# Scores of a local attention in one fp32 pass or in three fp32r passes, 128 or 256 keys wide

## The chip, the cores and the metric

The kernel runs on one core of a Trainium2 chip. The metric is the device time of one execution in microseconds (us). Engines are called by the names of the profile: PE is TensorE, PEld its weight load, DVE is VectorE, ACT is ScalarE, POOL is GpSimd, SP is SyncE, which here issues DMA transfers. Each engine works through its own list of instructions in order. They wait for each other by semaphores.

## The reference, cut to what matters

The program computes two transformer blocks, one after the other, on 512 tokens of width 1024. The first block has a gated mixer with a delta rule, cross attention over 256 memory rows and an MLP. The second block starts with eight projections of the same normalised input, among them q (8 heads of 64), k and v (2 heads of 64). The change is in its local attention:

```
q = apply_rope(q.reshape(b, s, 8, 64), cos, sin)
k = apply_rope(k.reshape(b, s, 2, 64), cos, sin)
# 4 blocks of 128 queries; each sees its own 128 keys and the 128 before them
scores = einsum('bnqhgd,bnkhd->bnhgqk', qb, kk) * 64 ** -0.5
scores = where(band & not_pad, scores, -inf)
m = maximum(max(scores), sink)
p = exp(scores - m);  denom = sum(p) + exp(sink - m)
out = einsum('bnhgqk,bnkhd->bnqhgd', p / denom, vv)
```

Beside it run a convolution branch (projections cb, cc, cx) and the gates. All products with weights are made in three passes over high and low parts: an fp32 number x is split into x_hi (rounded to fp32r) and x_lo = x - x_hi, and hi*hi + lo*hi + hi*lo is added up in one PSUM bank.

## The kernel before, in words

`schedule()` writes the order of all steps by hand as one list of (kind, number). Every engine walks through this list and does its own part of each kind, so a step's place in the list is its place on every engine that it touches.

Weights come as units of up to eight 128x128 tiles. For unit j, SP loads the raw weights, the step `split` makes w_hi on ACT (L1574), `low` makes w_lo on DVE (L1867), and `mm` is 24 matmuls of 128x512 on PE (L1272 to L1274). A split stands in the list three units ahead of its mm. The result lies in one of four PSUM banks until DVE takes it out (L1851, "leave").

Around the change the units are k2, q2 0, v2, q2 1 to 3, then cc2, cx2 and cb2 for each of eight tiles. After q2 n is out, ACT adds its bias (step `leave_q`, L1770), `rotate` n makes the rotated half in four copies on ACT (L1779, L1780), and `turned` n multiplies and adds on DVE (L2228, L2229, L2232). Two heads of each of the two key groups lie in one tile q2[:, n, :]: partitions 0 to 63 hold the head of group 0, partitions 64 to 127 that of group 1. k2 is one such tile.

`scores` n is one of 16 steps: PAIRS gives (block, pair, group), so that steps come in twos, one for each group. PE does both groups of a batch at the first of the two: for the two heads i of the pair and both groups, one fp32 matmul (L1530) of 64 partitions by 128 queries against 128 keys (block 0) or 256 keys (blocks 1 to 3). There are 8 such batches, of 4 matmuls each, and the trace records each fp32 matmul as two. DVE then adds the mask, takes the maximum and adds the sink (L2253 to L2262), ACT takes Exp (L1794, L1797) and DVE sums and inverts (L2264, L2266). Pairs 0 and 1 of the q2 tiles are tiles 0, 1 and tiles 2, 3. So batch 1 (scores 0 and 1) needs q2 0 and 1, and batch 2 (scores 2 and 3) needs q2 2 and 3. Batch 1 stands after mm cx2 0, batch 2 after mm cc2 1, with mm cb2 0 between them. PE waits with `turned_dve` before a batch.

Of the kernel before, what the change touches and what calls it, by code (L numbers as in the profile page):

```python
# [8 lines left out]
F32 = mybir.dt.float32  # L9
# [6 lines left out]
P = 128  # L16
# [177 lines left out]
def schedule():  # L194
# [3 lines left out]
    def add(kind, n=0):  # L198
        out.append((kind, n))
# [223 lines left out]
    for n in range(1, QT):  # L423
        project("q2", n)
        add("leave_q", n)
        if n == 1:
            add("value_turn")
        else:
            add("rotate", n - 1)
        if n != 2:  # L430
            add("turned", n // 2)

    def window_attention():
        for g in range(KVH):
# [14 lines left out]
    def conv_branch():  # L449
        for n in range(KT):  # L450
            project("cc2", n)
            add("cc", n)
            if n == 0:
                add("rotate", QT - 1)
                add("turned", QT - 2)
            yield
            project("cx2", n)
            add("cx", n)
            if n == 0:
                add("turned", QT - 1)  # L460
            yield
            project("cb2", n)
            add("cb", n)
            add("normed", n)
            add("b", (B_CONV, n))
            yield
        for n in range(KT):
            project("gc2", n)
            add("gate_c", n)
            yield  # L470
            project("conv_out2", n)
            add("conv_out", n)
            yield
# [282 lines left out]
def build_program(nc, x_in, mem_in, front_in, logits_in, weights_in, ws_in, columns_in, rows_in, sinks_in, matrices_in,  # L756
                  positions_in, out):
    with ExitStack() as base:
# [23 lines left out]
        sinks = sbuf("sinks", [P, QH])  # L782
        matrices = sbuf("matrices", [P, N_MATRICES, P])
        rstd = sbuf("rstd", [P, S])
        square_sum = sbuf("square_sum", [P, S])
        squares = [sbuf(f"square{i}", [P, S]) for i in range(2)]
        narrow = sbuf("narrow", [P, 16, H * NC])
        wide = [sbuf(f"temp{i}", [P, PAD + S]) for i in range(5)]
# [5 lines left out]
        k_low, v_low = ExitStack(), ExitStack()  # L794
        mem_k_lo = [sbuf("mem_k_early_lo", [P, EARLY_KEYS, M], F32R, stack=k_low)]
        k_low.close()
        mem_k_early = sbuf("mem_k_early", [P, EARLY_KEYS, M])
        banks = [base.enter_context(nc.psum_tensor(f"bank{i}", [P, S], F32)) for i in range(8)]

# [50 lines left out]
        second = ExitStack()  # L850
        rope_cos = sbuf("rope_cos", [P, S], stack=second)
        rope_sin = sbuf("rope_sin", [P, S], stack=second)
        q2 = sbuf("q2", [P, QT, S], stack=second)
        k2 = sbuf("k2", [P, S], stack=second)
        v2 = sbuf("v2", [P, NC, P], stack=second)
# [52 lines left out]
        def side(name, n=0):  # L908
            return banks[BANKS + SIDES.slot[name, n]][:, :]
# [86 lines left out]
        leave_q_dve, leave_q_act = signal("leave_q_dve", "leave_q"), signal("leave_q_act", "leave_q")  # L996
        rotate_act, rotate_dve, turned_dve = signal("rotate_act", "rotate"), signal("rotate_dve", "turned"), signal("turned_dve", "turned", 2)
        normed_dve = signal("normed_dve", "normed")
        value_dve, value_act = signal("value_dve", "value"), signal("value_act", "value")
        value_turn_pe, value_turn_act = signal("value_turn_pe", "value_turn"), signal("value_turn_act", "value_turn")  # L1000
        scores_pe, scores_dve, scores_act, scores_pool = (
# [176 lines left out]

        def summed(g):
            return square_dve.at((g, KT - 1)) if g in ON_DVE else square_pool.at((g, KT - 1))  # L1180

        def window(count):

# [6 lines left out]
        def tensor_program(pe):  # L1190
# [22 lines left out]
            for kind, n in SCHEDULE:  # L1213
# [283 lines left out]
                elif kind == "attend_turn":  # L1497
                    q.wait_ge(*attend_dve.at(n))
                    for c in range(MC):
                        bank = side("attend_turn", (n, c))  # L1500
                        wait_side("attend_turn", (n, c))
                        for s in range(NC):
                            t = pe.transpose(bank[:, chunk(s)], probs[n % 2][:, s, chunk(c)], eye)
                        t.then_inc(attend_turn_pe.handle, 1)
                elif kind == "attend_out":
                    q.wait_ge(*attend_low_dve.at(n // XT))
                    q.wait_ge(*mem_split_dve.at(3))
                    wait_side("attend_out", n)
                    for c in range(MC):
                        v_hi, v_lo = mem_v_hi[:, c, chunk(n)], mem_v_lo[:, c, chunk(n)]  # L1510
                        pe.matmul(side("attend_out", n), v_hi, probs_hi[:, c, :], start=c == 0, stop=False)
                        pe.matmul(side("attend_out", n), v_hi, probs_lo[:, c, :], start=False, stop=False)
                        t = pe.matmul(side("attend_out", n), v_lo, probs_hi[:, c, :], start=False, stop=c == MC - 1)
                    t.then_inc(attend_out_pe.handle, 1)
                elif kind == "value_turn":
                    q.wait_ge(*value_act.at())
                    wait_side("value_turn")
                    for c in range(NC):
                        t = pe.transpose(side("value_turn")[:, chunk(c)], temp("value")[:, chunk(c)], eye)
                    t.then_inc(value_turn_pe.handle, 1)  # L1520
                elif kind == "scores" and n % KVH == 0:
                    q.wait_ge(*turned_dve.at(QT))
                    q.wait_ge(*turned_dve.at(2 * window(n)[2] + 1))
                    for g in range(KVH):
                        wait_side("scores", n + g)
                    for i in range(2):
                        for count in range(n, n + KVH):
                            block, g, pair, halves, width, part = window(count)
                            b = side("scores", count)[:, 0:2 * width].rearrange("p (h k) -> p h k", h=2)
                            t = pe.matmul(b[:, i, :], q2[part, 2 * pair + i, chunk(block)], k2[part, (block + 1) * P - width:(block + 1) * P],  # L1530
                                          start=True, stop=True)
                            if i == 1:
                                t.then_inc(scores_pe.handle, 1)
                elif kind == "turn_probs":
                    block, g, pair, halves, width, part = window(n)
                    s = scores2[n % (2 * KVH)][:, 0:2 * width].rearrange("p (h k) -> p h k", h=2)
                    b = side("turn_probs", n)[:, 0:2 * width].rearrange("p (a h q) -> p a h q", a=halves, h=2)
                    q.wait_ge(*scores_pool.at(n))
                    wait_side("turn_probs", n)
                    for a in range(halves):  # L1540
                        for i in range(2):
                            t = pe.transpose(b[:, a, i, :], s[:, i, chunk(a)], eye)  # L1542
                    t.then_inc(turn_probs_pe.handle, 1)
                elif kind == "attended":
                    halves = window(n * PER_BLOCK)[3]
                    bank = side("attended", n)
                    q.wait_ge(*turn_probs_act.at((n + 1) * PER_BLOCK - 1))
                    q.wait_ge(*value_turn_act.at())
                    wait_side("attended", n)
                    for a in range(halves):  # L1550
                        for g in range(KVH):
                            part = slice(g * HD, (g + 1) * HD)
                            t = pe.matmul(bank[part, :], v2[:, n - halves + 1 + a, part], probs2_t[g][:, a, :, :].rearrange("p h q -> p (h q)"),  # L1553
                                          start=a == 0, stop=a == halves - 1)
                    t.then_inc(attended_pe.handle, 1)

        def scalar_program(act):
# [7 lines left out]
            for kind, n in SCHEDULE:  # L1565
# [201 lines left out]
                elif kind == "leave_q":  # L1767
                    to = q2[:, n, :] if n < QT else k2[:, :]
                    q.wait_ge(*leave_q_dve.at(n))
                    act.activation(to, to, ACT.Identity, bias=column("b_q", n) if n < QT else column("b_k")).then_inc(leave_q_act.handle, 1)  # L1770
                elif kind == "rotate":
                    to, other = q2[:, n, :] if n < QT else k2[:, :], temp("other", n)
                    free = temp_free("other", n)
# [58 lines left out]
        def vector_program(dve):  # L1832
# [29 lines left out]
            for kind, n in SCHEDULE:  # L1862
# [361 lines left out]
                elif kind == "turned":  # L2224
# [5 lines left out]
                    q.wait_ge(*rotate_dve.at(n))  # L2230
                    q.wait_ge(*turned_dve.at(n, 1))
                    dve.tensor_tensor(to, to, other, ALU.add).then_inc(turned_dve.handle, 1)  # L2232
                elif kind == "normed":
                    q.wait_ge(*row_act.at(A_SECOND, 2))
                    q.wait_ge(*stage_act.at((A_SECOND, n)))
# [7 lines left out]
                elif kind == "scores":  # L2243
                    block, g, pair, halves, width, part = window(n)
                    s = scores2[n % (2 * KVH)][:, 0:2 * width].rearrange("p (h k) -> p h k", h=2)
                    b = side("scores", n)[:, 0:2 * width].rearrange("p (h k) -> p h k", h=2)
                    biggest, bias, total, sink, inverse = (soft2[n % (2 * KVH)][:, i, :] for i in range(5))
                    own_sinks = sinks[:, g * QT + 2 * pair:g * QT + 2 * pair + 2]
                    q.wait_ge(*scores_pe.at(n))
# [275 lines left out]
```

## Time and profile before

| what | value |
|---|---|
| time, median of 3 runs | 1540.81 us (1540.01 to 1544.46) |
| time of the profiled execution | 1540.12 us |
| its span | 1538.4 us |
| PE busy | 1527.9 us, 99% of the span |
| DVE busy | 890.5 us, 58% |
| ACT busy | 616.2 us, 40% |
| POOL busy | 102.6 us, 7% |
| DMA | 146.70 MB, mean 95 GB/s |

The span runs from the first to the last instruction of the trace; 1.7 us of the execution lie outside it. A matmul's record reaches from its start to its modelled end, and consecutive ones overlap, so the pace of PE is read from the distances between starts and not from the durations.

### The profile page before, as it was taken

Reading aid. Unit: us, or ns where it says so; the run is one execution under the profiler, and the core shown is the slowest. Engines: PE = TensorE matmul, PEld = TensorE weight load, DVE = VectorE, ACT = ScalarE, POOL = GpSimd, SP = SyncE. Lnnn points to the kernel's source line nnn. Section 1 sums busy time; section 2 is a strip of 40 time slices with the busy share of each in tenths; the row PEclk is TensorE's granted clock in tenths of the full one; section 3 lists DMA queues with packets and bytes.
Section 4 is the critical chain, followed back from the end, with each engine's and each line's share of the span. In section 5 each row is a group of like instructions: output and inputs, shape, how many; then the busy total and the mean of one; then the engine's idle time right before and its main releaser. Section 6 shows DMA issues by size and latency. Waiting matters only on the chain.

```text
span 1538.4 us, 20544 instructions
## 1 busy us (share of the span) xinstructions
PE 1527.9 (99%) x8182; PEld 1270.6 (83%) x8182; DVE 890.5 (58%) x1356; ACT 616.2 (40%) x995; POOL 102.6 (7%) x87
## 2 busy tenths in 40 slices
PE   9999999999999999999999999999999999999998
PEld 7888889888888888888888877877888888888887
DVE  7777766666554343446556777644565653664565
ACT  6546334544443231323455443533343331332333
POOL 0000202110110000000230000100011000000000
PEclk9999999999999999999999999999999999999999
DMA  7111213421123232232222232221332322223212
GB/s 271 56 70 35 78 69 128 174 96 69 62 103 109 83 107 98 83 111 88 98 94 83 83 110 82 97 83 62 117 109 83 110 96 97 96 96 105 87 63 75
DMA packets 44861, 146.70 MB, mean 95 GB/s; under 512 B 4960, under 2 KB 8288, under 8 KB 44640
## 3 DMA queue, kind: packets, MB, share of 16 engines
q1 hardware_dynamic: 42592, 141.93, 26.3%
q10 hardware_dynamic: 2176, 3.47, 0.7%
q8 instruction: 65, 1.06, 0.3%
q14 instruction: 28, 0.23, 0.0%
HBM read 143.29 MB, written 2.10 MB: 95 GB/s over the span
## 4 chain that ended last, share of the span: by engine, by line
PE 94%; DVE 2%; issue 1%; DMA 1%; ACT 1%; POOL 0%; POOLq 0%; DVEq 0%; ACTq 0%; SPq 0%
PE bank L1272 28%; PE bank L1274 28%; PE bank L1273 28%; DMA xs<-x_in 1%; PE bank L1401 1%; DVE w_lo L1867 1%; PE bank L1427 1%; PE bank L1432 1%; PE bank L1530 0%; PE bank L1553 0%; PE bank L1542 0%; DVE xs L2152 0%; PE bank L1202 0%; PE bank L1218 0%; PE bank L1224 0%
## 5 line engine op out<-in xcount | busy, mean ns | idle before, releaser
L1272 PE MATMUL bank<-a_hi,w_hi 128*128 128x512 f32 (+1 forms) x1275 | 496.7, 390 | 0.0
L1274 PE MATMUL bank<-a_hi,w_lo 128*128 128x512 f32 (+1 forms) x1275 | 489.9, 384 | 0.0
L1273 PE MATMUL bank<-a_lo,w_hi 128*128 128x512 f32 (+1 forms) x1275 | 489.6, 384 | 0.0
L1867 DVE TENSOR_TENSOR w_lo<-w_raw,w_hi 128x1024 fp32r<-128x1024 f32 (+2 forms) x259 | 326.4, 1264 | 139.4 <-ACT w_hi L1574 138.8
L1574 ACT ACTIVATE w_hi<-w_raw 128x1024 fp32r<-128x1024 f32 (+2 forms) x259 | 266.2, 1034 | 203.9 <-PE bank L1274 195.3
L1272 PEld LDWEIGHTS bank<-a_hi,w_hi 128*128 128x128 f32 x1275 | 239.6, 188 | 49.5 <-issue 2.6
L1274 PEld LDWEIGHTS bank<-a_hi,w_lo 128*128 128x128 f32 x1275 | 239.5, 188 | 47.9
L1273 PEld LDWEIGHTS bank<-a_lo,w_hi 128*128 128x128 f32 x1275 | 239.7, 188 | 45.6 <-issue 0.2
L1272 PE MATMUL bank<-b_hi,w_hi 128*128 128x512 f32 (+1 forms) x720 | 275.9, 383 | 0.0
L1273 PE MATMUL bank<-b_lo,w_hi 128*128 128x512 f32 (+1 forms) x720 | 275.1, 382 | 0.0
L1274 PE MATMUL bank<-b_hi,w_lo 128*128 128x512 f32 (+1 forms) x720 | 275.1, 382 | 0.0
L1272 PEld LDWEIGHTS bank<-b_hi,w_hi 128*128 128x128 f32 x720 | 135.3, 188 | 26.7 <-issue 0.7
L1274 PEld LDWEIGHTS bank<-b_hi,w_lo 128*128 128x128 f32 x720 | 135.3, 188 | 26.2
L1273 PEld LDWEIGHTS bank<-b_lo,w_hi 128*128 128x128 f32 x720 | 135.4, 188 | 25.9
L2152 DVE TENSOR_TENSOR xs<-xs,bank 128x512 f32<-128x512 f32 (+1 forms) x88 | 55.8, 635 | 125.8 <-PE bank L1274 118.9
L1851 DVE TENSOR_TENSOR temp<-bank,rstd 128x512 f32<-128x512 f32 x109 | 74.7, 686 | 71.9 <-PE bank L1274 62.8
L1859 DVE SCALAR_TENSOR_TENSOR temp<-temp,columns 128x512 f32<-128x512 f32 x96 | 72.2, 752 | 28.6 <-ACT temp L1823 17.2
L2353 POOL TENSOR_TENSOR square_sum<-square_sum,square 128x512 f32<-128x512 f32 x28 | 39.5, 1410 | 615.4 <-ACT square L1609 615.4
L2130 DVE TENSOR_TENSOR b_lo<-temp,b_hi 128x512 fp32r<-128x512 f32 x62 | 42.9, 692 | 59.3 <-ACT b_hi L1717 59.0
L1717 ACT ACTIVATE b_hi<-temp 128x512 fp32r<-128x512 f32 x62 | 39.2, 632 | 83.9 <-DVE temp L2322 58.2
L1766 ACT ACTIVATE temp<-temp 128x512 f32<-128x512 f32 x32 | 20.2, 632 | 93.2 <-DVE temp L2218 93.2
L2344 POOL TENSOR_TENSOR narrow<-narrow,columns 128x4 f32<-128x4 f32 (+1 forms) x13 | 19.4, 1495 | 410.6 <-DVE narrow L1910 373.9
(334 smaller groups left out, 1239.5 us busy)
## 6 DMA issues: line engine op xcount, KB each, us to landing
w_raw<-weights_in SPq DMA_DIRECT2D x247, 512.0 KB, 3.2
w_raw<-weights_in SPq DMA_DIRECT2D x8, 384.0 KB, 2.9
x_first<-x_in SPq DMA_DIRECT2D x8, 256.0 KB, 5.9
xs<-x_in ACTq DMA_DIRECT2D x2, 1024.0 KB, 10.4
w_raw<-weights_in SPq DMA_DIRECT2D x8, 256.0 KB, 2.6
mem_x<-mem_in SPq DMA_DIRECT2D x1, 1024.0 KB, 8.1
out<-xs SPq DMA_DIRECT2D x8, 128.0 KB, 1.7
w_raw<-front_in SPq DMA_DIRECT2D x5, 192.0 KB, 6.2
```

Source lines behind the costliest of these rows:

```text
L1272: pe.matmul(to, weights_hi[:, at], hi, start=k == k0, stop=False)
L1273: pe.matmul(to, weights_hi[:, at], lo, start=False, stop=False)
L1274: t = pe.matmul(to, weights_lo[:, at], hi, start=False, stop=k == k1 - 1)
L1574: act.activation(split_weights(n)[0][:, 0:size], raw[:, n % SLOTS, 0:size], ACT.Copy).then_inc(split_act.handle, 1)
L1717: act.activation(b_hi[:, b_slot(g, i), :], x, ACT.Copy).then_inc(b_act.handle, 1)
L1766: act.activation(temp("relu", n), temp("relu", n), ACT.Square).then_inc(relu_act.handle, 1)
L1851: return dve.tensor_tensor(to, full(name, n, k0)[0:to.shape[0], 0:width], scale[0:to.shape[0], 0:width], ALU.mult)
L1859: dve.scalar_tensor_tensor(acc, buf[:, at:at + S], weight(i), acc, ALU.mult, ALU.add).then_inc(done.handle, 1)
L1867: dve.tensor_tensor(lo[:, 0:size], raw[:, n % SLOTS, 0:size], hi[:, 0:size].bitcast(F32), ALU.subtract).then_inc(split_dve.handle, 1)
L2130: dve.tensor_tensor(lo, x, hi.bitcast(F32), ALU.subtract).then_inc(b_dve.handle, 1)
L2152: dve.tensor_tensor(xs[:, t, tokens], xs[:, t, tokens], full(name, t, k0)[:, 0:tokens.stop - tokens.start], ALU.add).then_inc(residual_dve ...
L2353: pool.tensor_tensor(total, total, square("square", n)[:, 0:total.shape[1]], ALU.add).then_inc(square_pool.handle, 1)
```

## The change

Five new tiles hold high parts and low parts of q2 and k2. The low parts take the address of q2 and k2 themselves, the high parts that of tiles with other uses at other times. The step `half_high` n copies a turned tile to fp32r on ACT, `half_low` n subtracts it on DVE; n is 0 to 3 for q2 and 4 (QT) for k2. The steps stand in the hand-written list as the diff shows. PE waits for `half_low` of the tiles where it waited for `turned`, and makes each score in three fp32r matmuls, 256 keys wide in block 0 too, with the two groups in turn within each pass.

```
@@ schedule(), loop over n = 1 to QT-1 of q2
         if n == 1:
             add("value_turn")
         else:
+            add("half_low", (QT, 0)[n - 2])
             add("rotate", n - 1)
-        if n != 2:
+        if n == 2:
+            add("half_high", 0)
+        else:
             add("turned", n // 2)
+        if n == 1:
+            add("half_high", QT)
@@ conv_branch()
             project("cc2", n)
             add("cc", n)
             if n == 0:
+                add("half_high", 1)
                 add("rotate", QT - 1)
                 add("turned", QT - 2)
+                add("half_low", 1)
             yield
             project("cx2", n)
             add("cx", n)
             if n == 0:
+                add("half_high", 2)
                 add("turned", QT - 1)
+                add("half_low", 2)
+                add("half_high", QT - 1)
             yield
             project("cb2", n)
             add("cb", n)
+            if n == 0:
+                add("half_low", QT - 1)
             add("normed", n)
...
+        half_high_act, half_low_dve = continued(gate_act, "half_high"), continued(decay_dve, "half_low")
...
+        def scored(n):
+            if n == QT:
+                return k2_hi[:, :], k2_lo[:, :], k2[:, :]
+            return q2_hi[n // 2][:, n % 2, :], q2_lo[:, n, :], q2[:, n, :]
...
@@ tensor_program()
                 elif kind == "scores" and n % KVH == 0:
-                    q.wait_ge(*turned_dve.at(QT))
-                    q.wait_ge(*turned_dve.at(2 * window(n)[2] + 1))
+                    q.wait_ge(*half_low_dve.at(QT))
+                    q.wait_ge(*half_low_dve.at(2 * window(n)[2] + 1))
...
                     for i in range(2):
-                        for count in range(n, n + KVH):
-                            block, g, pair, halves, width, part = window(count)
-                            b = side("scores", count)[:, 0:2 * width].rearrange("p (h k) -> p h k", h=2)
-                            t = pe.matmul(b[:, i, :], q2[part, 2 * pair + i, chunk(block)], k2[part, (block + 1) * P - width:(block + 1) * P],
-                                          start=True, stop=True)
-                            if i == 1:
-                                t.then_inc(scores_pe.handle, 1)
+                        block, _, pair = window(n)[0:3]
+                        first = max(block - 1, 0) * P
+                        q_hi, q_lo, _ = scored(2 * pair + i)
+                        k_hi, k_lo, _ = scored(QT)
+                        for at, (one, other) in enumerate(((q_hi, k_hi), (q_hi, k_lo), (q_lo, k_hi))):
+                            for count in range(n, n + KVH):
+                                part = window(count)[5]
+                                b = side("scores", count).rearrange("p (h k) -> p h k", h=2)
+                                t = pe.matmul(b[:, i, :], one[part, chunk(block)], other[part, first:first + 2 * P], start=at == 0, stop=at == 2)
+                                if i == 1 and at == 2:
+                                    t.then_inc(scores_pe.handle, 1)
@@ scalar_program()
+                elif kind == "half_high":
+                    high, low, whole = scored(n)
+                    q.wait_ge(*turned_dve.at(n))
+                    act.activation(high, whole, ACT.Copy).then_inc(half_high_act.handle, 1)
@@ vector_program()
+                elif kind == "half_low":
+                    high, low, whole = scored(n)
+                    q.wait_ge(*half_high_act.at(n))
+                    dve.tensor_tensor(low, whole, high.bitcast(F32), ALU.subtract).then_inc(half_low_dve.handle, 1)
```

The semaphore of `half_low` is the one that the first block used under the name decay_dve, that of `half_high` is gate_act.

On PE, batch 2 of the scores (between mm cc2 1 and mm cx2 1). Before:

```order
L1273 MATMUL bank<-a_lo,w_hi 128x512
L1274 MATMUL bank<-a_hi,w_lo 128x512
L1530 MATMUL bank<-k,q 128x128 [waits value_turn_act,row_act,turned_dve]
L1530 MATMUL bank<-k,q 128x128 x3
L1272 MATMUL bank<-a_hi,w_hi 128x512 [waits cc_dve,split_dve,split_act]
```

Now:

```order
L1305 MATMUL bank<-a_lo,w_hi 128x512
L1306 MATMUL bank<-a_hi,w_lo 128x512
L1567 MATMUL bank<-k_hi,q_late_hi 128x256 [waits value_turn_act,row_act,decay_dve]
L1567 MATMUL bank<-k_hi,q_late_hi 128x256
L1567 MATMUL bank<-k_lo,q_late_hi 128x256 x2
L1567 MATMUL bank<-k_hi,q_lo 128x256 x2
L1567 MATMUL bank<-k_hi,q_late_hi 128x256 x2
L1567 MATMUL bank<-k_lo,q_late_hi 128x256 x2
L1567 MATMUL bank<-k_hi,q_lo 128x256 x2
L1304 MATMUL bank<-a_hi,w_hi 128x512 [waits cc_dve,split_dve,split_act]
```

Four matmuls become twelve at the same place, and the wait is for decay_dve, that is `half_low` 3, in place of `turned` 3.

On DVE, what follows the softmax of scores 1 (RECIPROCAL is its last instruction). Before:

```order
L2266 RECIPROCAL soft_1<-soft_1 128x2 [waits scores_dve]
L1867 TENSOR_TENSOR w_lo<-w_raw,w_hi 128x1024 [waits split_act]
L1851 TENSOR_TENSOR temp<-bank,rstd 128x512 [waits mm_pe]
L2289 SCALAR_TENSOR_TENSOR temp<-temp,columns 128x512 [waits cb_dve,cx_dve]
L2238 SCALAR_TENSOR_TENSOR xs<-xs,columns,rstd 128x512 [waits square2_act,square_act,row_act]
```

Now:

```order
L2310 RECIPROCAL soft_1<-soft_1 128x2 [waits scores_dve]
L1907 TENSOR_TENSOR w_lo<-w_raw,w_hi 128x1024 [waits split_act]
L1891 TENSOR_TENSOR temp<-bank,rstd 128x512 [waits mm_pe]
L2333 SCALAR_TENSOR_TENSOR temp<-temp,columns 128x512 [waits cb_dve,cx_dve]
L2276 TENSOR_TENSOR q_lo<-q,q_late_hi 128x512 [waits gate_act]
L2282 SCALAR_TENSOR_TENSOR xs<-xs,columns,rstd 128x512 [waits square2_act,square_act,row_act]
```

The new row L2276 is `half_low` 3. It stands behind both softmaxes of batch 1, one w_lo and the leave and bias of cb2 0.

On ACT, from the weights of unit cx2 1 to the first Exp. Before:

```order
L1574 ACTIVATE w_hi<-w_raw 128x1024 [waits mm_pe,raw_landed2]
L1808 ACTIVATE temp<-temp,columns 128x512 [waits cx_dve]
L1810 ACTIVATE temp<-temp,columns 128x512 [waits cx_dve]
L1794 ACT_TABLE_LOAD
L1794 ACTIVATE scores_0,soft_0<-scores_0,soft_0 128x128 [waits scores_dve]
```

Now:

```order
L1610 ACTIVATE w_hi<-w_raw 128x1024 [waits mm_pe,raw_landed2]
L1848 ACTIVATE temp<-temp,columns 128x512 [waits cx_dve]
L1850 ACTIVATE temp<-temp,columns 128x512 [waits cx_dve]
L1810 ACTIVATE q_late_hi<-q 128x512 [waits turned_dve] x2
L1834 ACT_TABLE_LOAD
L1834 ACTIVATE scores_0,soft_0<-scores_0,soft_0 128x128 [waits scores_dve]
```

`half_high` 2 and 3 (L1810 x2) now stand between L1850 and the table load for Exp, and the second of them waits for `turned` 3.

## Rows read from the trace of the kernel before

**Rows 1.** The page: busy time of the engines, and the chain that ended last.

```profile
PE 1527.9 (99%) x8182; PEld 1270.6 (83%) x8182; DVE 890.5 (58%) x1356; ACT 616.2 (40%) x995; POOL 102.6 (7%) x87
...
PE 94%; DVE 2%; issue 1%; DMA 1%; ACT 1%; POOL 0%; POOLq 0%; DVEq 0%; ACTq 0%; SPq 0%
```

**Rows 2.** Waits of PE: waited in total us, times, longest us.

```profile
PE bank L1212 <- DVE warm L1834: 1.3, 1, 1.3
...
PE bank L1401 <- DVE inv_tb L2085: 0.5, 1, 0.5
```

**Rows 3.** Groups by line and form: busy us, mean ns, idle before.

```profile
L1530 PE MATMUL bank<-k,q 64*128 64x256 f32 x48 | 6.8, 402 | 0.0
```

**Rows 4.** Timeline of PE at batch 1: start us, duration us, instruction.

```profile
828.64 0.39 PE L1274 MATMUL bank<-a_hi,w_lo 128*128 128x512 f32 x1
828.96 0.72 PE L1530 MATMUL bank<-k,q 64*128 64x128 f32 x8
829.61 0.50 PE L1272 MATMUL bank<-a_hi,w_hi 128*128 128x512 f32 x1
```

**Rows 5.** Timeline of PE at batch 2.

```profile
840.72 0.71 PE L1530 MATMUL bank<-k,q 64*128 64x128 f32 x8
```

**Rows 6.** Timeline of PE at batch 3, the first of block 1.

```profile
863.84 1.14 PE L1530 MATMUL bank<-k,q 64*128 64x256 f32 x8
864.90 0.50 PE L1272 MATMUL bank<-a_hi,w_hi 128*128 128x512 f32 x1
```

**Rows 7.** Timeline of PE, fp32 matmuls over all 128 rows.

```profile
142.08 0.39 PE L1442 MATMUL bank<-inv_t,strict_t 128*128 128x128 f32 x2
142.31 0.39 PE L1443 MATMUL bank<-decays_t,inv_t 128*128 128x128 f32 x2
```

**Rows 8.** Timeline of PE, fp32r matmuls of 256 columns, the last of them.

```profile
1529.23 0.28 PE L1273 MATMUL bank<-b_lo,a_hi 128*128 128x256 f32 x1
1529.35 0.28 PE L1274 MATMUL bank<-b_hi,a_lo 128*128 128x256 f32 x1
```

**Rows 9.** Timeline of DVE; in brackets idle time before and its releaser.

```profile
818.35 1.23 DVE L1867 TENSOR_TENSOR w_lo<-w_raw,w_hi 128x1024 fp32r<-128x1024 f32 x1 [4.46 <-ACT w_hi L1574]
...
827.77 0.69 DVE L2232 TENSOR_TENSOR q<-q,temp 128x512 f32<-128x512 f32 x1
828.38 1.22 DVE L1867 TENSOR_TENSOR w_lo<-w_raw,w_hi 128x1024 fp32r<-128x1024 f32 x1
...
835.38 0.69 DVE L2232 TENSOR_TENSOR q<-q,temp 128x512 f32<-128x512 f32 x1
...
843.76 0.75 DVE L2289 SCALAR_TENSOR_TENSOR temp<-temp,columns 128x512 f32<-128x512 f32 x1
844.43 0.75 DVE L2238 SCALAR_TENSOR_TENSOR xs<-xs,columns,rstd 128x512 f32<-128x512 f32 x1
```

**Rows 10.** Timeline of ACT: w_hi of unit cb2 0, the table load for Exp, Exp.

```profile
817.26 1.06 ACT L1574 ACTIVATE w_hi<-w_raw 128x1024 fp32r<-128x1024 f32 x1
...
832.52 1.28 ACT L1794 ACT_TABLE_LOAD   x1
837.29 0.40 ACT L1794 ACTIVATE scores<-scores,soft 128x128 f32<-128x128 f32 x1 [3.49 <-DVE soft L2260]
```

**Rows 11.** The page: a subtraction on DVE and a copy on ACT, 128x512.

```profile
L2130 DVE TENSOR_TENSOR b_lo<-temp,b_hi 128x512 fp32r<-128x512 f32 x62 | 42.9, 692 | 59.3 <-ACT b_hi L1717 59.0
L1717 ACT ACTIVATE b_hi<-temp 128x512 fp32r<-128x512 f32 x62 | 39.2, 632 | 83.9 <-DVE temp L2322 58.2
```

**Rows 12.** Timeline of ACT: a table load whose function is wanted at once.

```profile
38.56 1.28 ACT L1667 ACT_TABLE_LOAD   x1
39.86 0.22 ACT L1667 ACTIVATE small<-small 128x16 f32<-128x16 f32 x1
```

**Rows 13.** Timeline of PE at the start: fp32 matmuls after idleness.

```profile
1.25 4.72 PE L1212 MATMUL bank<-warm 128*128 128x128 f32 x22 [1.25 <-DVE warm L1834]
```

**Rows 14.** Windows at the end: us, busy by engine (x), granted clock, DMA, GB/s.

```profile
1534.70:1538.00 3.30, 0.00 (x0) 0.00 (x0) 0.47 (x1) 0.00 (x0) 0.00 (x0) 0.50 0.83 274
```

More of the change, by code:

```diff
@@ L784, in build_program @@
         rstd = sbuf("rstd", [P, S])
+        scores_d = ExitStack()
+        k2_hi = sbuf("k2_hi", [P, S], F32R, stack=scores_d)
+        scores_d.close()
         square_sum = sbuf("square_sum", [P, S])
+        scores_b = ExitStack()
+        q2_hi = [sbuf("q2_late_hi", [P, 2, S], F32R, stack=scores_b)]
+        scores_b.close()
         squares = [sbuf(f"square{i}", [P, S]) for i in range(2)]
@@ L796, in build_program @@
         k_low.close()
+        scores_a = ExitStack()
+        q2_hi.insert(0, sbuf("q2_early_hi", [P, 2, S], F32R, stack=scores_a))
+        scores_a.close()
         mem_k_early = sbuf("mem_k_early", [P, EARLY_KEYS, M])
@@ L852, in build_program @@
         rope_sin = sbuf("rope_sin", [P, S], stack=second)
+        scores_c = ExitStack()
+        q2_lo = sbuf("q2_lo", [P, QT, S], F32R, stack=scores_c)
+        k2_lo = sbuf("k2_lo", [P, S], F32R, stack=scores_c)
+        scores_c.close()
         q2 = sbuf("q2", [P, QT, S], stack=second)
@@ L2245, in vector_program @@
                     s = scores2[n % (2 * KVH)][:, 0:2 * width].rearrange("p (h k) -> p h k", h=2)
-                    b = side("scores", n)[:, 0:2 * width].rearrange("p (h k) -> p h k", h=2)
+                    b = side("scores", n).rearrange("p (h k) -> p h k", h=2)[:, :, 0:width]
                     biggest, bias, total, sink, inverse = (soft2[n % (2 * KVH)][:, i, :] for i in range(5))
```

## The prediction

> **What bounds the kernel now.** I read the page first, then the waits of PE, then the timelines of PE, DVE and ACT around the first batches of scores. PE is busy 99% of the span and 94% of the chain that ended last is PE's [rows 1]. It has six waits of its own in the whole trace. They fall from 1.3 us to 0.5 us, at the start, the end and in the first block, and none is near the attention [rows 2]. So PE's order and pace set the time: time taken from PE is gained, and any wait put on PE is lost in full, since nothing behind it has slack to give back. DVE and ACT matter only where PE waits for them.
>
> **What PE's scores cost before.** One batch is 8 records. For 128 keys the batch starts at 828.96 and the next unit at 829.61, so it takes 0.65 us [rows 4]. For 256 keys it goes from 863.84 to 864.90, 1.06 us [rows 6]. Over all rows of the array, two fp32 records of 128 columns go by each 0.22 to 0.23 us (142.08 to 142.31), 0.11 us each [rows 7]. Eight records of 256 columns would need 8 x 0.22 = 1.8 us one after the other, and the batch took 1.06. So the two groups, on different halves of the rows, ran side by side: four steps, each of two records. The steps are worth (1.06 - 0.65) / 4 = 0.10 us per 128 columns, so 0.21 us for 256 keys and 0.10 us for 128. The rest of a batch, about 0.23 us, and the 0.32 us from the last L1274 (828.64) to the batch's start [rows 4] come from going over to half-height tiles and back.
>
> Here the Trainium skill has a rule (TensorEngine Tiling (Array Packing), Key Properties): changing the tiling mode drains the engine, and tiles of one mode load and multiply independently. The trace agrees with it: 0.32 us from the start of a 512-column matmul to the batch [rows 4], where two of 256 columns take 0.24 [rows 8]. Both ends of a batch change mode before and after, so the rule takes nothing from the sum.
>
> **What PE's scores cost after.** Twelve fp32r matmuls of 256 columns, in six steps of two if the groups run side by side again. The nearest row is the full-height fp32r matmul of 256 columns: 1529.23 to 1529.35, 0.12 us apart [rows 8]. Six steps are 0.72 us. Against four steps of 0.21 (0.84 us) that saves 0.12 us in each of the six batches of blocks 1 to 3, 0.7 us in all. In block 0 it costs 0.72 - 0.42 = 0.3 us for each of two batches, because they become 256 keys wide. No row shows fp32r on half-height tiles. The cheap bound is that found above. The dear bound is twelve matmuls one after the other, 1.44 us. I take the cheap one, since the fp32 records on the same tiles did overlap. The fp32 batch's group of 48 records is only 6.8 us of busy time [rows 3], so the matmuls alone can't move much either way.
>
> **What ACT and DVE get.** Five copies on ACT, and five subtractions on DVE. The nearest rows are the copy to b_hi, 0.63 us, and the subtraction to b_lo, 0.69 us [rows 11]. Behind each other they cost 0.61 us, as from 827.77 to 828.38 on DVE [rows 9]; I use 0.6 for both. Summed they are 3 us on each, which neither engine would feel over the kernel. But here the two hand work to each other, and PE waits for the last of it. I follow the list.
>
> Step one, up to batch 1. `half_high` of k and of q2 0 stand on ACT ahead of the w_hi at 817.26 [rows 10]. ACT is the late one there: DVE stood idle 4.46 us for that w_hi before it began w_lo at 818.35 [rows 9]. So both copies count: +1.2 us for everything behind on both engines. The subtractions for k and q2 0 fall into DVE's waits for ACT and cost nothing; without that cover they would add up to 1.2 us. The add that ends `turned` 2 stood at 827.77 to 828.46 [rows 9]. With +1.2 it ends at 829.66. `half_low` 1 starts where w_lo started, at 828.38 + 1.2 = 829.58, and ends 0.69 us later at 830.3. Batch 1 started at 828.96 [rows 4] and now waits until 830.3. That is a first wait of about 1.3 us.
>
> Step two, from batch 1 to batch 2. `half_low` 1 and the copy of `half_high` 1 push the next w_lo and all behind it by another 0.6 us, to +1.8. `turned` 3, whose add ended at 835.38 + 0.69 = 836.07 [rows 9], ends at 837.9. Behind it DVE has `half_low` 2, to +2.4 for the softmax of scores 0. On ACT `half_high` 3 waits for 837.9 and ends at 838.5. Only then comes the table load, 1.28 us long, which had lain in ACT's idle time at 832.52 with 3.49 us of waiting behind it [rows 10]. It ends at 839.85, and Exp starts there, not at 837.29: +2.6. From there DVE and ACT alternate through both softmaxes, the w_lo of cb2 1 and the leave of cb2 0, with little waiting for anything else, so +2.6 holds down to L2289, which was at 843.76 [rows 9]. `half_low` 3 takes the place of L2238, at 844.43 + 2.6 = 847.0, and ends at 847.7.
>
> Before, batch 2 needed `turned` 3 alone, done at 836.07, and started at 840.72 [rows 5], with 4.6 us to spare. Now it needs an instruction that stands behind both softmaxes. PE arrives at 840.72 + 1.3 + 0.3 = 842.3 and starts batch 2 at 847.75: a second wait of 5.4 us. PE is then 7.0 us late (847.75 - 840.72), which holds the first wait and the wider batch 1.
>
> The Trainium skill (ScalarE: Activation LUTs, What ACT_TABLE_LOAD costs) says that a switch of tables costs a drain of about 1.38 us beside the load of about 1.28 us. That would put Exp, and batch 2, 1.4 us later still, and the time up by that. The trace speaks against it: a load from 38.56 to 39.84 was followed by its own ACTIVATE at 39.86 [rows 12], so the sum has 1.28 us alone.
>
> Behind batch 2 PE is 7.0 us later than before and DVE only about 3.2 us (2.6 and the subtraction), so PE waits for it no more. SP's loads of weights wait for splits that come up to 2.6 us later, three units (some 16 us) ahead of their use.
>
> **The clock.** Batch 2's wait is the first long idleness of PE in the middle of the kernel. At the end of the trace the granted clock is 0.50, the lower of the two levels (1.2 of 2.4 GHz) [rows 14], some 5 us after the last dense matmul at 1529.35 [rows 8]. At the start, after idleness, 22 records took 4.72 us, 4.35 without the last one's tail [rows 13]; at 0.11 us each [rows 7] they would take 2.4. If the clock falls in the wait, coming back costs about that difference, 1.9 us. Bounds are 0 (it doesn't fall) and 3.8 (twice as long at the lower level). With 5.4 us of idleness against 5 us at the end, I think it falls, and take 1.9.
>
> **Sum.** 7.0 (both waits) + 0.3 (batch 2 wider) - 0.7 (six batches) + 1.9 (clock) = 8.5 us. Against the profiled execution, 1540.12 us, that is 1548.6. Its time is 0.7 us below the median of the runs shown, which I leave out of the sum and inside the range.
>
> **The rivals.**
> A: as above, 1548.6.
> B: both waits, but the clock holds: 1546.7. For it: the 5.4 us are only a little more than the 5 us between the last dense matmul and the lower clock at the end, and my wait could come out shorter.
> C: both waits, and fp32r groups on half-height tiles don't overlap. Then seven batches (2 to 8) take 0.72 us more each, 5.0 us: 1551.7 without the clock's share and 1553.6 with it. Against it stands the overlap of the fp32 records.
> D, the other side: DVE has `half_low` 3 ready before PE gets to batch 2. It decides at 842.3: the step would have to stand or run 5.4 us earlier than I have it. Then the scores save 0.7 and cost 0.6 in block 0, and the first wait alone is left or gone: 1540.0 to 1541.4, no change. Against it stand the rows of the list, where `half_low` 3 is behind RECIPROCAL, w_lo, leave and L2333, and DVE can't overtake.
> E, the drain behind the table load. If Exp can't start when the load ends but some time later, `half_low` 3 and batch 2 come later by that time, as both softmaxes stand between. The rows give no such time (39.84 to 39.86, [rows 12]), and the bound from them is 0.02 us, 1548.6 again. By the price in the Trainium skill named above the time would be 1550.0.
> The change also doesn't make PE faster beyond D: a gain over 0.3% would need 4.6 us, and all the scores' steps before are 6 x 0.84 + 2 x 0.42 = 5.9 us.
>
> **How the numbers follow.** A 0.44, B 0.27, C 0.12, D 0.10, E 0.02, and 0.05 for anything else, more than half of it faster. The forecast is A. A measurement of this kernel tells 0.3%, 4.6 us, from no change, so slower begins at 1545.4. A, C and E lie above it, and B mostly (0.22 of 0.27, since a second wait 1.3 us shorter would bring it inside). That makes slower 0.79, same 0.18, faster 0.03. The range goes from 1544.5, which holds B with a wait 2 us shorter, to 1552.5, which holds A with the dear clock and C without.
>
> **What the profile after would show.** Two waits of PE at the new L1567, one of about 1.3 us near 829 and one of about 5.4 us near 842, both for DVE q_lo at L2276. Exp of scores 0 near 839.9, right behind the end of the table load. The granted clock below 1.00 in the microseconds behind 847. Batches of blocks 1 to 3 about 0.94 us from start to the next unit, and records in pairs. The prediction is wrong if the second wait is under 3 us, if the batches take 1.6 us, or if PE waits again behind batch 2.

## The result, and the profile after

| | before | after |
|---|---|---|
| median time | 1540.78 us | 1549.21 us (1548.71 to 1549.88, 6 runs) |
| profiled execution | 1540.12 us | 1549.88 us |
| its span | 1538.4 us | 1548.1 us |
| PE busy | 1527.9 us | 1530.5 us |
| mean granted clock | 0.999 | 0.996 |

The ratio is 1.0051 (95% interval 1.0039 to 1.0064): slower, by 8.4 us or 0.5%. Timed again later (e10), the changed kernel took 1550.04 us against 1540.85, ratio 1.0057. The forecast was 1548.6 us.

PE's waits, changed kernel (engine and line, releaser: us in total, times, longest), answer to [rows 2]:

```profile
PE bank L1567 <- DVE q_lo L2276: 6.5, 2, 5.3
PE bank L1244 <- DVE warm L1874: 1.3, 1, 1.3
PE bank L1234 <- POOL narrow L2388: 1.0, 1, 1.0
PE bank L1250 <- ACT w_hi L1613: 0.9, 1, 0.9
```

The first row is new: both waits for `half_low`, and nothing else in the attention. The last row lies at 6.4 us. From the start to batch 1 PE has the same work in all kernels here, yet it came out 0.4 us later in this trace than in that of before. The eleven traces other than that of before are later there by 0.2 to 1.5 us. So traces are compared below by distances inside the attention, not by their ends. The timeline of PE at batch 1 and batch 2 (start us, duration us; in brackets idle time before) answers to [rows 4, 5]:

```profile
829.06 0.39 PE L1306 MATMUL bank<-a_hi,w_lo 128*128 128x512 f32 x1
830.62 0.39 PE L1567 MATMUL bank<-k_hi,q_early_hi 64*128 64x256 f32 x2 [1.17 <-DVE q_lo L2276]
...
831.53 0.50 PE L1304 MATMUL bank<-a_hi,w_hi 128*128 128x512 f32 x1
...
842.32 0.39 PE L1306 MATMUL bank<-a_hi,w_lo 128*128 128x512 f32 x1
847.99 0.58 PE L1567 MATMUL bank<-k_hi,q_late_hi 64*128 64x256 f32 x2 [5.28 <-DVE q_lo L2276]
848.37 0.42 PE L1567 MATMUL bank<-k_lo,q_late_hi 64*128 64x256 f32 x2
...
849.57 0.80 PE L1304 MATMUL bank<-a_hi,w_hi 128*128 128x512 f32 x1
```

The last matmul ahead of batch 2 started at 842.32, and batch 2 at 847.99, 5.7 us behind it, where 0.32 us is usual [rows 4]. Batch 1 took 0.91 us; batch 2, behind the long wait, 1.58 us, with 0.21 us between steps in place of 0.12. The windows around it (us, busy PE, PEld, DVE, ACT, POOL with counts, granted clock, DMA share, GB/s) tell why:

```profile
842.70:847.60 4.90, 0.01 (x1) 0.00 (x0) 3.32 (x7) 2.14 (x7) 0.61 (x1) 1.00 0.08 23
847.70:854.40 6.70, 6.41 (x23) 5.20 (x24) 5.62 (x15) 2.22 (x7) 0.61 (x1) 0.50 0.38 135
854.60:860.00 5.40, 5.40 (x26) 4.44 (x25) 3.10 (x7) 2.65 (x7) 0.61 (x1) 1.00 0.19 52
```

The clock was at its lower level (1.2 GHz, 0.50) for the 6.7 us of that window, and PE worked in nearly all of it. It was not so in the second trace of the same kernel (e10 below), and that matters for the price. On ACT, before the first Exp:

```profile
838.17 0.63 ACT L1810 ACTIVATE q_late_hi<-q 128x512 fp32r<-128x512 f32 x1 [3.09 <-DVE q L2272]
838.82 1.28 ACT L1834 ACT_TABLE_LOAD   x1
840.11 0.40 ACT L1834 ACTIVATE scores<-scores,soft 128x128 f32<-128x128 f32 x1
```

Before, ACT waited 3.49 us behind its table load [rows 10]; now the load itself is what Exp waits for. And on DVE, the step for which batch 2 waits, which answers to the last two of [rows 9]:

```profile
846.58 0.75 DVE L2333 SCALAR_TENSOR_TENSOR temp<-temp,columns 128x512 f32<-128x512 f32 x1
847.25 0.69 DVE L2276 TENSOR_TENSOR q_lo<-q,q_late_hi 128x512 fp32r<-128x512 f32 x1
```

It ended at 847.94, and PE started 0.05 us later. Of the 9.8 us between the two spans, 0.4 us lie before batch 1, 6.9 us are the later start of batch 2 (18.93 us behind the L1306 of 829.06, where it was 12.08 us behind the L1274 of 828.64), 3.2 us lie between batch 2 and batch 3, and the rest of the attention gives back 0.75 us.

### The profile page after: what moved, and what is told of

It reads as the page before. It is cut to its first block, busy times and chain, and to the rows that moved or that the text cites. A ratio compares the mean times of both kernels' runs of the same rounds, so it can differ in the third digit from the quotient of the medians.

```text
span 1548.1 us, 20618 instructions
## 1 busy us (share of the span) xinstructions
PE 1530.5 (99%) x8214; PEld 1273.8 (82%) x8214; DVE 894.0 (58%) x1361; ACT 619.1 (40%) x1000; POOL 102.4 (7%) x87
## 4 chain that ended last, share of the span: by engine, by line
PE 93%; DVE 2%; ACT 2%; issue 2%; DMA 1%; SPq 0%; POOLq 0%; DVEq 0%; POOL 0%
PE bank L1304 28%; PE bank L1306 28%; PE bank L1305 28%; PE bank L1433 1%; PE bank L1459 1%; PE bank L1464 1%; DVE w_lo L1907 1%; PE bank L1274 0%; PE bank L1272 0%; PE bank L1273 0%; PE bank L1567 0%; PE bank L1589 0%; PE bank L1578 0%; ACT w_hi L1610 0%; DMA w_raw<-weights_in 0%
## 5 line engine op out<-in xcount | busy, mean ns | idle before, releaser
L1306 PE MATMUL bank<-a_hi,w_lo 128*128 128x512 f32 (+1 forms) x1275 | 490.7, 385 | 0.0
L1306 PEld LDWEIGHTS bank<-a_hi,w_lo 128*128 128x128 f32 x1275 | 240.1, 188 | 48.3
L1306 PE MATMUL bank<-b_hi,w_lo 128*128 128x512 f32 (+1 forms) x720 | 275.1, 382 | 0.0
L1306 PEld LDWEIGHTS bank<-b_hi,w_lo 128*128 128x128 f32 x720 | 135.3, 188 | 26.2
```

Source lines behind the costliest of these rows:

```text
L1306: t = pe.matmul(to, weights_lo[:, at], hi, start=False, stop=k == k1 - 1)
```

## The experiments

Two theories stood against each other. By the first, only waits cost: PE waits for `half_low` because of where the steps stand, and the clock falls in the longer wait, or behind it. By the second, the added work costs, on ACT and DVE or on PE, wherever it stands. Medians below stand beside that of before on the same chip.

**e1: the step for batch 2 early.**

```
@@ conv_branch(), behind project("cx2", 0)
                 add("half_low", 2)
                 add("half_high", QT - 1)
+                add("half_low", QT - 1)
@@ behind project("cb2", 0)
-            if n == 0:
-                add("half_low", QT - 1)
```

> The changed kernel with one step moved: half_low 3 stands right behind half_low 2 and half_high 3, ahead of the softmax of scores 0, instead of behind the leave of cb2 0. Same instructions. Theory (waits): q_lo 3 ends near 839.6, before PE comes to batch 2 near 842.3, so the wait of 5.3 us goes, and with it the stretch at the lower clock (about 3 us). The first wait of 1.2 us stays. Expected 1541.6 us (1540.8 before, +1.3 first wait, +0.5 block 0 wider, -1.0 shorter batches in blocks 1 to 3). Rival (work): the ten added instructions are what costs, wherever they stand; expected 1548 to 1549 us. Rival (matmuls): the fp32r passes cost the time; expected above 1545 us.

Measured: 1542.54 us against 1540.72, ratio 1.0013 (1.0004 to 1.0022). The only wait of PE for q_lo is the first one:

```profile
PE bank L1566 <- DVE q_lo L2275: 1.2, 1, 1.2
```

One moved step, with all instructions kept, took back 6.6 of 8.4 us. Work and matmuls as causes of the bulk are out, and the granted clock in its trace is 1.00 from 820 to 900 us. The time stayed 0.9 us over the expectation. The trace has two candidates and can't settle their share of the median: PE was already 1.1 us later than in the trace of before ahead of batch 1, and it lost 0.3 us more at unit cb2 3, of which e4 says why. One of the eleven executions took 1547.54 us with a mean clock of 0.996; it has no trace.

**e2: the same step in the middle.** `half_low` 3 behind both softmaxes, ahead of low of cb2 1:

```
@@ conv_branch()
+            if n == 0:
+                add("half_low", QT - 1)
             project("cb2", n)
             add("cb", n)
-            if n == 0:
-                add("half_low", QT - 1)
```

> The changed kernel with half_low 3 right behind both softmaxes of batch 1, ahead of the w_lo and the leave of cb2 0. A dose between the changed kernel and the first experiment: the wait before batch 2 should be about 2.1 us in place of 5.3. Theory (waits, and the clock falls only after long idleness): 3.2 us less of waiting and 3.1 us less at the lower clock, 1542.9 us, granted clock 1.00 around 846 us. Rival (the clock falls after any wait of 2 us): 1546.0 us, with a stretch at 0.50. Rival (work): 1548 to 1549 us.

Measured: 1544.81 us against 1540.72, ratio 1.0029 (1.0018 to 1.0040). The wait was 2.0 us:

```profile
PE bank L1567 <- DVE q_lo L2276: 3.2, 2, 2.0
```

The profiled execution (1544.19 us) kept its clock (1.00 from 845 to 852 us), and its 23.42 us from batch 2 to batch 3 (845.16 to 868.58) are those of e5, which has no wait (23.41). So this wait cost its own length and nothing behind it. But the eight executions stood on two levels: four at 1543.4 to 1544.2 us with a mean granted clock of 0.998 or 0.999, four at 1545.4 to 1547.1 us with 0.997. I take it that the clock fell in those four; they have no trace, so this is read from the mean alone. My expectation had one level, and the waits' theory missed the median by 1.9 us, the rival by 1.2: the lower level lies near the first, the upper one at the second.

**e3: the work without the wait.** PE and the mask as before the change, all steps of ACT and DVE kept:

```
@@ tensor_program(), vector_program()
-  (three fp32r passes, 256 keys, waits for half_low_dve)
+  (one fp32 pass, 128 or 256 keys, waits for turned_dve, as before the change)
-                    dve.tensor_tensor(low, whole, high.bitcast(F32), ALU.subtract)
+                    dve.tensor_tensor(high, whole, high.bitcast(F32), ALU.subtract)
```

> The scores as before the change (fp32, one pass, block 0 128 keys wide, PE waiting for turned), but ACT and DVE still make all half_high and half_low steps at the changed kernel's places. Nobody uses their results: half_low writes over the high part, so that q2 and k2 stay whole. Theory (waits): turned 3 ends near 838.1, before PE needs it at 840.7, and nobody waits for the rest; 1540.8 us, same as before, though the softmaxes of batch 1 come 2.8 us later. Rival (work): the ten instructions, 6.6 us of busy time, delay splits and leaves; expected 1543 to 1548 us.

Measured: 1542.53 us against 1540.72, ratio 1.0014 (1.0005 to 1.0023). That is neither expectation: no wait before a batch, and still 1.8 us. The timeline of PE has a new wait, for which the view names no releaser ("issue"). The next matmul starts 1.63 us behind the last one, where 0.23 is usual, so 1.4 us are lost:

```profile
882.46 0.39 PE L1306 MATMUL bank<-a_hi,w_lo 128*128 128x512 f32 x1
884.09 0.47 PE L1304 MATMUL bank<-a_hi,w_hi 128*128 128x512 f32 x1 [1.24 <-issue]
```

**e4: both steps early.** e1, and `half_high` 1 and `half_low` 1 behind `turned` 1:

```
@@ schedule(), behind add("half_high", QT) in the loop over q2
+        if n == QT - 1:
+            add("half_high", 1)
+            add("half_low", 1)
@@ conv_branch(), behind add("cc", 0)
-                add("half_high", 1)
...
-                add("half_low", 1)
```

> The first experiment's kernel with half_high 1 and half_low 1 also moved, to right behind turned 1 (ahead of the w_hi and w_lo of cc2 1, where DVE waits for ACT anyway). Theory (waits): q_lo 1 ends near 826.4, before PE comes to batch 1 near 829, so the first wait goes too. What is left is the price of the matmuls: +0.5 us in block 0, -1.0 us in blocks 1 to 3; expected 1540.3 us, same as before the change or a little under it. Rival (matmuls): above 1543 us. Rival (work): 1548 us.

Measured: 1541.99 us against 1540.72, ratio 1.0013 (1.0004 to 1.0022). Both waits before the scores are gone, and the wait of e3 is there again, with the full matmul change in:

```profile
882.24 0.39 PE L1306 MATMUL bank<-a_hi,w_lo 128*128 128x512 f32 x1
883.87 0.47 PE L1304 MATMUL bank<-a_hi,w_hi 128*128 128x512 f32 x1 [1.25 <-issue]
```

The unit that starts late is cb2 3, and it needs its w_lo. Timeline of DVE, e4, and below it the kernel before, where the last line is PE's first matmul of this unit:

```profile
882.15 1.61 DVE L1907 TENSOR_TENSOR w_lo<-w_raw,w_hi 128x1024 fp32r<-128x1024 f32 x1 [0.59 <-ACT w_hi L1610]
```

```profile
878.97 1.61 DVE L1867 TENSOR_TENSOR w_lo<-w_raw,w_hi 128x1024 fp32r<-128x1024 f32 x1 [0.59 <-ACT w_hi L1574]
...
881.82 0.39 PE L1272 MATMUL bank<-a_hi,w_hi 128*128 128x512 f32 x1
```

Before, w_lo of cb2 3 ended at 880.58 and PE began the unit at 881.82: 1.24 us to spare. In e4 DVE had not caught up in the 40 us since the softmaxes of batch 1 and was still 3.2 us late, so w_lo ended at 883.76 and PE waited. In the changed kernel PE was itself 10 us late there, and the lateness of DVE didn't show.

**e5: that w_lo early too.** e4, and:

```
+def ahead(schedule_out):
+    j = PROJ["cb2", 3, 0]
+    moved = [("split", j), ("low", j)]
+    out = [s for s in schedule_out if s not in moved]
+    at = out.index(("scores", 4))
+    return out[:at] + moved + out[at:]
-SCHEDULE = schedule()
+SCHEDULE = ahead(schedule())
```

> The kernel of e4 (both half_low steps early, no wait before the scores) with one more move: split and low of unit cb2 3 stand ahead of the softmax of scores 4 and 5, not behind it. The trace of e4 showed PE idle 1.2 us at 882.3 us until that w_lo was made, because DVE's list was still 3.2 us late there and the unit's margin was 1.3 us. Theory (lateness of DVE, used up by the first margin that is smaller): the 1.2 us go; expected 1540.8 us, the same as before the change. Rival (the wait comes from elsewhere, or moves on to the next unit): 1542 us as e4.

Measured: 1540.55 us against 1541.01, ratio 0.9998 (0.9989 to 1.0007), and no wait of PE in the attention. The w_lo of cb2 3 now began at 876.06:

```profile
876.06 1.22 DVE L1916 TENSOR_TENSOR w_lo<-w_raw,w_hi 128x1024 fp32r<-128x1024 f32 x1
```

The whole loss is gone with every instruction of the change in place, as far as 0.1% can be told. Against the changed kernel five steps stand elsewhere, in three moves: `half_high` 1 with `half_low` 1, `half_low` 3, and split with low of cb2 3.

**e6: e3 with the same move of cb2 3.** Edit: `SCHEDULE = ahead(schedule())` of e5, in e3.

> The kernel of e3 (fp32 scores as before the change, with all half_high and half_low steps made and not used) with the same move of the unit cb2 3. e3 came out 1.8 us over before, of which its trace shows 1.2 us as the wait at 882.5. Theory: the wait goes, expected 1541.2 us. Rival (the added instructions cost by themselves): 1542.5 us.

Measured: 1540.62 us against 1541.01, ratio 0.9998 (0.9990 to 1.0007). The wait is gone from the trace, so the five copies and five subtractions cost nothing by themselves that the times can tell. The 1.4 us that e3's trace lost were that one margin. Against the kernel before on each chip the move takes 2.2 us off the median (1.8 over it, then 0.4 under it). The 0.8 us between them aren't traced; they may be the spread between sets of runs.

**e7: the groups one after the other.** e5, and in the PE part:

```
-                        for at, (one, other) in enumerate(((q_hi, k_hi), (q_hi, k_lo), (q_lo, k_hi))):
-                            for count in range(n, n + KVH):
+                        for count in range(n, n + KVH):
+                            for at, (one, other) in enumerate(((q_hi, k_hi), (q_hi, k_lo), (q_lo, k_hi))):
```

> The kernel of e5 with the twelve matmuls of a batch in another order: for each head all three passes of group 0, then all three of group 1, not the two groups in turn within a pass. If PE takes matmuls strictly in order and two on the same rows can't overlap, each batch has ten or so steps of 0.12 us in place of six (only the last of group 0 and the first of group 1 side by side): about 0.4 us more a batch, 3.5 us in all, 1544.3 us. If the order doesn't matter (each half of the rows goes on by itself): as e5, 1540.8 us.

Measured: 1540.96 us against 1541.01, ratio 0.9999 (0.9990 to 1.0008). The program has three matmuls of group 0 and then three of group 1 for each head. The timeline of PE at batch 3 shows them in twos of the same kind:

```profile
864.91 0.40 PE L1576 MATMUL bank<-k_hi,q_early_hi 64*128 64x256 f32 x2
865.14 0.28 PE L1576 MATMUL bank<-k_lo,q_early_hi 64*128 64x256 f32 x2
865.25 0.28 PE L1576 MATMUL bank<-k_hi,q_lo 64*128 64x256 f32 x2
...
865.82 0.50 PE L1313 MATMUL bank<-a_hi,w_hi 128*128 128x512 f32 x1
```

If the compiled program keeps the order of the source, which the trace can't show, PE did not take the matmuls one by one in that order. The batch took 0.91 us, as in e5 (865.90 to 866.80, 0.90). Taking the groups in turn within each pass, as the change does, gains nothing.

**e8: block 0 narrow.** e5, and in the PE part:

```
-                        first = max(block - 1, 0) * P
+                        first, wide_by = max(block - 1, 0) * P, window(n)[4]
-  t = pe.matmul(b[:, i, :], one[part, chunk(block)], other[part, first:first + 2 * P], ...
+  t = pe.matmul(b[:, i, 0:wide_by], one[part, chunk(block)], other[part, first:first + wide_by], ...
```

> The kernel of e5 with block 0 of the scores 128 keys wide again, in fp32r (batches 1 and 2 only; columns 128 to 255 of these score tiles are neither made nor read). If a step of 128 columns is bound by its 64x128 weight load or by its columns, it takes 0.06 to 0.11 us in place of 0.117, and batches 1 and 2 take 0.5 to 0.85 us in place of 0.91: 0.1 to 0.8 us less than e5. Rival (fp32r is no faster per column below 256 columns and falls back to the pace of fp32): steps of 0.11 us or more, no gain or a loss, time as e5.

Measured: 1540.62 us against 1541.01, ratio 0.9999 (0.9991 to 1.0008). Timeline of PE at batch 1 of e8:

```profile
830.04 0.33 PE L1576 MATMUL bank<-k_hi,q_early_hi 64*128 64x128 f32 x2
830.21 0.28 PE L1576 MATMUL bank<-k_lo,q_early_hi 64*128 64x128 f32 x2
830.32 0.28 PE L1576 MATMUL bank<-k_hi,q_lo 64*128 64x128 f32 x2
...
830.86 0.50 PE L1313 MATMUL bank<-a_hi,w_hi 128*128 128x512 f32 x1
```

Steps of 128 columns are 0.11 us apart, those of 256 columns 0.117; the batch took 0.82 us (830.04 to 830.86) in place of 0.90. So half the columns save 0.08 us a batch, 0.16 us in all, below what the times can tell. Whether the weight load or a slower pace of narrow fp32r matmuls holds the step at 0.11 us stays open; widening block 0 costs next to nothing either way.

**e9: a wait between 2.0 and 5.3 us.** The changed kernel with `half_low` 3 between low of cb2 1 and the leave of cb2 0:

```
             project("cb2", n)
+            if n == 0:
+                add("half_low", QT - 1)
             add("cb", n)
-            if n == 0:
-                add("half_low", QT - 1)
```

> The changed kernel with half_low 3 behind the w_lo of cb2 1 but ahead of the leave and bias of cb2 0: a wait before batch 2 of about 3.9 us, between the 2.0 us of e2 (clock stayed at 1.00 in its trace) and the 5.3 us of the changed kernel (clock fell). By waits alone: before +1.3 +0.5 -1.0 +3.9, 1545.7 us on the scale of 1541.0 before, if the clock stays; about 1548.7 us with some 3 us more if it falls as in the changed kernel. I expect that it falls in part of the executions only, so times on two levels some 2 to 3 us apart, and a median of 1546 to 1547 us.

Measured: 1547.35 us against 1540.85, ratio 1.0037 (1.0025 to 1.0049), with a wait of 3.8 us and, from within it on, the lower clock:

```profile
PE bank L1567 <- DVE q_lo L2276: 5.0, 2, 3.8
```

```profile
843.30:845.20 1.90, 0.00 (x0) 0.00 (x0) 0.44 (x4) 1.82 (x6) 0.55 (x1) 1.00 0.00 0
845.30:852.00 6.70, 4.96 (x20) 4.09 (x21) 6.30 (x9) 1.58 (x2) 0.00 (x0) 0.50 0.24 79
```

PE's wait ended at 847.04, so 1.8 us of the low stretch lay inside it. I expected the fall in part of the executions. The mean clock was 0.996 or 0.997 in all seven, as in the changed kernel, so I take it that it fell in each; one of them has a trace. The mean alone is no proof of where it fell: of the 74 executions of the kernel before that were timed beside these experiments, one shows 0.997 (1545.11 us) and one 0.996 (1546.52 us), without any such wait.

**e10: the changed kernel again.**

> The changed kernel itself again, on the same chip as e9. All six executions so far were at 1548.7 to 1549.9 us with a mean granted clock of 0.996 to 0.997, where before has 0.999: the clock fell in every one. Expected again: median 1549.2 us, and in the trace a wait of 5.3 us before batch 2 with 6 to 8 us at 0.50 behind it.

Measured: 1550.04 us (1549.38 to 1553.86, five executions) against 1540.85, ratio 1.0057 (1.0041 to 1.0073), with the wait of 5.3 us as expected. The lower clock is there too, for some 6.8 us, but not all of it behind the wait:

```profile
843.30:846.00 2.70, 0.00 (x0) 0.00 (x0) 1.24 (x4) 1.92 (x6) 0.61 (x1) 1.00 0.00 0
846.10:852.80 6.70, 4.20 (x18) 3.52 (x19) 6.45 (x13) 1.61 (x3) 0.00 (x0) 0.50 0.36 112
```

Batch 2 started at 848.60. So 2.6 us of the low stretch passed while PE stood idle anyway, and PE worked 4.2 us of it, where it worked 6.4 us in the first trace.

## Why the prediction was right

By its steps:

- The first wait: 1.3 us predicted, 1.2 us measured.
- Batch 2's start: 7.0 us later predicted, 6.9 us measured in both traces, with a second wait of 5.3 us for 5.4. The chain behind it holds link by link. `turned` 3 ended at 838.13 (837.9 predicted), the table load at 840.10 (839.85), Exp began at 840.11, `half_low` 3 at 847.25 (847.0); 0.4 us of each is the later start of the whole kernel in that execution. e1 and e4 show the cause: moved steps alone remove the waits.
- Exp began 0.01 us after its table load. So the trace gives no drain behind the load, and the Trainium skill's 1.38 us (ScalarE: Activation LUTs, What ACT_TABLE_LOAD costs) did not come; rival E is out.
- The scores on PE: the groups overlapped, so rival C is out. A batch of blocks 1 to 3 went from 1.06 [rows 6] to 0.90 or 0.91 us, 0.16 us less. From one batch's start to the next start, against the same distance before, each of the six saved 0.11 to 0.14 us, 0.74 in all, where 0.12 and 0.7 were predicted; what eats the other 0.03 us a batch isn't traced. Batches of block 0 grew by 0.26 us for 0.3.
- The clock fell, as forecast. Its price was the largest miss in the first trace, and none in the second. From the start of batch 2 to that of batch 3, e5, with the same instructions and no wait, took 23.41 us (842.49 to 865.90). The changed kernel took 26.35 in its first trace (847.99 to 874.34), 25.26 in e10's (848.60 to 873.86), and e9 took 25.63 (847.04 to 872.67): 2.9, 1.85 and 2.2 us more, for the 1.9 of the sum with its bounds of 0 and 3.8. The low stretch was equally long in all three. What differed is when it began, 5.0, 2.7 and 2.0 us into the wait, and so for how long PE worked in it: 6.4, 4.2 and 5.0 us, at a price of about 0.45 us for each of them.
- That 1.9 is so near is luck in part. It was the surplus of a stretch at the start of the kernel in which the view gives a granted clock of 1.00, so the rows do not show that this is what coming back costs; and its records start from 1.25 to 5.70, 4.45 us and not 4.35. Nor did the sum ask how much of the low stretch would pass in the wait, where it costs nothing. And the prediction argued for the fall with 5.4 us of idleness against 5 us at the end; in two of the three traces the clock fell much sooner in the wait.
- The profiled sum misses by 1.3 us (9.8 for 8.5): 1.0 us is the clock and 0.4 us what the trace lost ahead of batch 1. The medians differ by 8.4 us. A small slip: the chances of the rivals add up to 0.80 for slower, not 0.79.

Two of its sentences were wrong though the time was right. Rival D said that without the waits the time would be 1540.0 to 1541.4. e1, with the first wait left, came to 1542.5, and e4, with none, to 1542.0. The prediction shows that DVE's lateness doesn't matter behind batch 2 with PE 7 us late, and takes this over to D, where PE isn't late. There it met a margin of 1.24 us at cb2 3, 40 us on. And B was given 0.27 because the wait seemed barely long enough; e9's mean clocks say that it fell in all seven executions after 3.8 us.

Rival D as a possibility for the finished schedule was true: with three moves of steps (e5) the change is worth nothing and costs nothing, 0.9998 (0.9989 to 1.0007). None of the versions is measurably faster than the kernel before.

## What to carry to other kernels

When a change lets the bottleneck engine wait for a new step, its price is set by what stands ahead of that step in its engine's list, not by the step's own 0.7 us. Follow that list link by link, including a table load that had been hidden. Where a busy engine is made late by some us, look for the smallest margin further on that hangs on it; removing the first wait can bring the next to light. A wait on TensorE can cost more than its own length, because of the lower clock behind it: here 1.9 to 2.9 us more for waits of 3.8 and 5.3 us, nothing more for the 2.0 us of e2's trace. And two traces of one kernel can differ by 1 us in that price, so one trace doesn't size it.

## What the runs showed of the hardware that I had not expected

- Two sets of matmuls on different halves of the rows went side by side even when the program gave three of one half before the first of the other (e7): the pairs start 0.010 us apart, and the batch takes 0.91 us. The trace before had this for fp32 already. There the two records of one matmul are given ahead of those of the other group, and the 8 records still ran in four steps of two, by the prediction's reading of [rows 6].
- The clock was at its lower level for some 6.8 us in each of the three traces with a wait of 3.8 or 5.3 us, from 2.0, 2.7 or 5.0 us into the wait. By the mean clock it fell in all 18 executions with such a wait. With a wait of 2.0 us (e2), 1.2 us of waiting some 13 us ahead of it, it stayed at 1.00 in the one trace, and by the two levels of times and mean clock it probably fell in four of eight executions.
- A table load on ACT was 1.28 us long, and the activation that wanted the table began 0.01 us after it.
- An fp32r step on half-height tiles takes 0.117 us for 256 columns (e5) and 0.11 us for 128 (e8).
